# Down matrices of the experts started from ScalarE's queue instead of the sync engine's

## What is computed

```python
weights = (g_w * e_w).reshape(-1)                       # 2 experts per token
expert = (g_idx * EXPERTS_PER_GROUP + e_idx).reshape(-1)
order = jnp.argsort(expert)
xs = t[order // EXPERT_TOPK]                            # 512 slots, sorted by expert
sizes = jnp.bincount(expert, length=N_EXPERTS)
hid = jax.nn.silu(lax.ragged_dot(xs, w_gate, sizes)) * lax.ragged_dot(xs, w_up, sizes)
out = lax.ragged_dot(hid, w_down, sizes) * weights[order][:, None]
```

## Time and profile before

| | us |
|---|---|
| median of 3 runs | 1532.62 (1530.26 to 1532.73) |
| the profiled execution | 1532.07 |
| its span in the trace | 1530.3 |
| TensorE busy (matmuls) | 1366.8, 89% |
| VectorE busy | 529.9, 35% |
| ScalarE busy | 359.4, 23% |
| GpSimd busy | 54.2, 4% |
| moved by the DMA engines | 360.95 MB, 236 GB/s over the span |

### The profile page before, as it was taken

The page is one execution under the profiler, slowest core; times in us unless marked ns, Lnnn a source line. Parts: engine busy times, 40 slices in busy tenths (PEclk is TensorE's granted clock), DMA queues, the critical chain, the costliest instruction groups (busy, mean ns, idle before and its releaser), DMA issues.

```text
span 1530.3 us, 19672 instructions
## 1 busy us (share of the span) xinstructions
PE 1366.8 (89%) x7747; PEld 1010.1 (66%) x7748; DVE 529.9 (35%) x890; ACT 359.4 (23%) x500; POOL 54.2 (4%) x93
## 2 busy tenths in 40 slices
PE   6978999989979699998799788958999999888887
PEld 5867999987647499998676567854444444333335
DVE  2563554436654254543302434242111111111111
ACT  2632433320243243331301354022000000000001
POOL 1000000000110100000000000000000000000010
PEclk9989999999999899999999899978999999999998
DMA  9634555438871745450834113140999999999992
GB/s 311 235 110 165 166 166 197 158 99 326 318 277 54 248 165 165 164 192 1 362 140 164 47 63 110 55 176 1 419 429 428 429 428 429 429 428 429 428 428 96
DMA packets 101168, 360.95 MB, mean 236 GB/s; under 512 B 4416, under 2 KB 51696, under 8 KB 88704
## 3 DMA queue, kind: packets, MB, share of 16 engines
q1 hardware_dynamic: 93344, 333.72, 56.4%
q0 software_dynamic: 7632, 26.44, 5.0%
q10 hardware_dynamic: 144, 0.11, 0.0%
HBM read 359.18 MB, written 1.07 MB: 235 GB/s over the span
## 4 chain that ended last, share of the span: by engine, by line
PE 71%; DMA 15%; DVE 9%; ACT 3%; issue 1%; POOL 0%; SPq 0%; POOLq 0%; DVEq 0%; ACTq 0%
PE ps L1380 17%; PE ps L1328 14%; DMA wbuf<-in_w_up 12%; PE ps L1647 10%; PE ps L1312 9%; PE ps L1659 4%; PE ps L1541 3%; PE ps L1319 3%; PE ps L1635 2%; DVE wbuf L999 2%; PE ps L1291 1%; DMA wbuf<-in_lru_w_in 1%; PE ps L1622 1%; DMA wbuf<-in_w_ada 1%; PE ps L1347 1%
## 5 line engine op out<-in xcount | busy, mean ns | idle before, releaser
L1380 PE MATMUL ps<-big_parts,parts 128*128 128x256 f32 x2112 | 261.8, 286 | 8.6 <-DVE big_parts L925 8.5
L1380 PEld LDWEIGHTS ps<-big_parts,parts 128*128 128x128 f32 x2112 | 259.2, 194 | 10.0 <-issue 9.3
L1647 PE MATMUL ps<-wbuf,big 128*64 128x512 f32 x1024 | 226.4, 593 | 14.2 <-DMA wbuf<-in_w_up 13.6
L1312 PE MATMUL ps<-big,wbuf 128*128 128x256 f32 x896 | 199.1, 385 | 11.8 <-DMA wbuf<-in_lru_w_in 4.6
L925 DVE TENSOR_TENSOR parts<-wbuf,parts 128x2048 fp32r<-128x2048 f32 x66 | 150.9, 2292 | 142.0 <-ACT parts L620 77.6
L1312 PEld LDWEIGHTS ps<-big,wbuf 128*128 128x128 f32 x896 | 172.8, 193 | 38.4 <-issue 9.4
L1647 PEld LDWEIGHTS ps<-wbuf,big 128*64 128x64 f32 x1024 | 84.6, 137 | 152.1 <-issue 145.8
L1328 PE MATMUL ps<-big_parts,parts 128*128 128x256 f32 x1056 | 134.1, 288 | 8.8 <-DVE parts L925 8.8
L1328 PEld LDWEIGHTS ps<-big_parts,parts 128*128 128x128 f32 x1056 | 131.9, 197 | 9.2 <-DVE parts L925 9.2
L1659 PE MATMUL ps<-wbuf,big 128*64 128x512 f32 x512 | 116.9, 597 | 19.5 <-DVE big L1257 19.5
L1255 DVE TENSOR_TENSOR big<-big,ps 128x256 f32<-128x256 f32 x32 | 13.5, 421 | 334.1 <-ACT big L814 334.1
(11 more groups left out here) (263 smaller groups left out, 1078.9 us busy)
## 6 DMA issues: line engine op xcount, KB each, us to landing
wbuf<-in_w_gate SPq DMA_DIRECT2D x32, 2048.0 KB, 25.2
wbuf<-in_w_up SPq DMA_DIRECT2D x32, 2048.0 KB, 29.6
wbuf<-in_w_down SPq DMA_DIRECT2D x32, 2048.0 KB, 29.3
wbuf<-in_ffn_w_in SPq DMA_DIRECT2D x44, 1024.0 KB, 9.4
wbuf<-in_w_ada POOLq DMA_DIRECT2D x12, 2048.0 KB, 12.0
wbuf<-in_ffn_w_out SPq DMA_DIRECT2D x22, 1024.0 KB, 5.1
wbuf<-in_w_in SPq DMA_DIRECT2D x10, 2048.0 KB, 8.0
wbuf<-in_attn_w_qkv SPq DMA_DIRECT2D x6, 2048.0 KB, 11.0
```

The lines of the kernel that those rows point to most:

```text
L1312: ins = mm(b[:, d * 256:(d + 1) * 256], w[:, k, (m + d) * P:(m + d + 1) * P], rhs[:, k], start=(k == 0), stop=(k == kn - 1))
L1380: ins = mm(ps[:, b, d * 256:(d + 1) * 256], w[pw][:, k, d * P:(d + 1) * P], h_part_of[px][:, k], start=(k == 0 and i == 0), stop=(k == KC ...
L1647: ins = mm(at, x[:, k], gu_place[s][:, :, k, h * 256:(h + 1) * 256], start=(k == 0), stop=(k == KC - 1))
```

## The change

The three down loads of `load_next` in SP's loop, and the two behind it, are taken out, together with SP's waits for `down_done`. ScalarE starts them instead, right behind its copy L816 of the same expert's result; the copy has waited for the same `down_done`. For that ScalarE's loop gets three experts in its body (slots are fixed addresses there too), nine times round for experts 0 to 26, and five experts written out behind it, the last three without a load. Gate and up stay with SP, and so do all three matrices of experts 0 to 2.

```diff
@@ -459,8 +459,6 @@
                 sp.wait_ge(gu_done[0], e + 1 + EXPERT_SLOTS)
                 load_gate_up(sp, s, e + EXPERT_SLOTS)
-                sp.wait_ge(down_done[0], e + 1)
-                load_down(sp, s, e + EXPERT_SLOTS)
@@ -817,12 +815,21 @@
             nc.scalar.nop().then_inc(y_ev[0], 1)
-            with act.Fori(0, N_EXP) as e:
+
+            def act_expert(e, s):
                 n_more, before_more = more_windows(act, e)
                 with act.If(n_more > 0), act.Fori(0, n_more) as w:
                     act_window(1, before_more + w)
                     act.wait_ge(more_done, before_more + w + 1)
                 act_window(0, e)
+                if s is not None:
+                    load_down(act, s, e + EXPERT_SLOTS)
+
+            with act.Fori(0, (N_EXP - EXPERT_SLOTS) // EXPERT_SLOTS) as j:
+                for s in range(EXPERT_SLOTS):
+                    act_expert(EXPERT_SLOTS * j + s, s)
+            for e in range(N_EXP - N_EXP % EXPERT_SLOTS - EXPERT_SLOTS, N_EXP):
+                act_expert(e, e % EXPERT_SLOTS if e + EXPERT_SLOTS < N_EXP else None)
```

## The result

The changed kernel takes 1538.36 us (median of 6 runs, 1536.1 to 1539.6), the one before 1531.78 in its 6 runs (1526.9 to 1532.73). The ratio, which is formed over all runs and not from the two medians, is 1.0045 with a 95% interval of 1.0031 to 1.0059: **slower**, by 4.7 to 9.0 us. The forecast was 1541.0, slower by 8.6 in the expert stage, within 1534 to 1547.

The account below looks back on a forecast made before the run. The expert stage's unbroken DMA stream was taken to bound the kernel. Terms 0 + 0 + 8.6 + 0 on 1532.07 us gave 1540.7, or 1541.2 against the median; forecast 1541.0 us, range 1534 to 1547.

Parts of the forecast that it names:

- What bounds the kernel: Expert stage: the DMA stream of weights never pauses, 14.68 us an expert; TensorE needs less, 13.43.
- (b): Expert stage: the later down issues open no hole in the stream; last matrix still lands about 1500.8; cost 0.
- The sum for the last byte: End of the expert stream: 1495 + 1.325/0.4285 puts the last byte at 1498.1 us.
- (a): Issue of downs on ScalarE: 0.6 to 0.7 us later, behind L816, covered by 6.27 us; cost 0, SP's saving 0.
- (c): Landing order: two queues share engines half and half, a down takes 9.8 us; downs run ahead, ups fall behind.
- The rival of one stream in effect: Both issuers' loads served in order asked for, down 31 landing last; not slower, 1532.1 to 1532.7 us; chance 0.12.
- (d): Stage end: up 31 lands last, 5.0 us later; TensorE's 13.43 pace after up 30 makes the last L1647 +8.6 us.
- just in time: Stage end: down 31, issued at 1476.1, is through at 1490.5, before up 30 lands at 1491.0.
- (e): Stream rate with two queues: bounded at +6.4 to -3.0 us on 425.8 us; taken as 0.
- the tail stays: Behind the last L1647: the work on TensorE, VectorE and ScalarE keeps its length.

Follow-up runs that it names:

- swap: Against the changed kernel, queues exchanged: ScalarE starts gate and up, SP starts down; 1539.50 us, ratio 1.0052 to the kernel before.
- last1: Against the kernel before, only the down load of expert 31 is moved to ScalarE's queue; 1536.09 us, ratio 1.0030.
- last2: Against the kernel before, only the down loads of experts 30 and 31 are moved to ScalarE's queue; 1540.88 us, ratio 1.0050.

## Why the prediction was right

**What bounds the kernel, and (b), no hole.** Right. The sum for the last byte gives 1498.1 in both traces.

**(a) The issue costs nothing.** Right, and sooner than expected. It does not stand behind the 0.60 us of the copy; ScalarE's rows of the changed kernel:

```profile
1157.37 0.60 ACT L814 ACTIVATE big<-ps 128x512 f32<-128x512 f32 x1 [6.17 <-PE ps L1666]
1157.51 0.35 ACTq L385 DMA_DIRECT2D wbuf<-in_w_down  x1
1164.24 0.38 ACT L812 ACTIVATE big<-ps 128x256 f32<-128x256 f32 x1 [6.27 <-PE ps L1654]
```

It begins 0.14 us after the copy begins, some 0.2 us later than SP's did and not 0.6 to 0.7, takes 0.35 instead of 0.41, and the next silu has its 6.27 us of idle time as in the earlier trace rows.

**(c) Half and half.** Right, nearly: 13.9 us of flight where 1.9 + 9.8 + 2.7 = 14.4 were expected, and swap shows the same with the roles exchanged. The queues show it directly, here while the last down flows (after, 1479.4 to 1488.6 us):

```profile
q1 hardware_dynamic: 146, 2.13, 54.4%
q10 hardware_dynamic: 126, 1.80, 46.0%
```

In last1, from 1469 to 1478 us, it is 1.87 MB on q1 and 2.03 on q10. This was the step with the thinnest evidence, a pair of one software and one hardware queue in short packets. The rival of one stream in effect fell with it. The Trainium skill's rule (DMA: Bandwidth & Descriptors, Issuing engines are not separate DMA queues) is that issuing from several engines saves only the issuer's time. For the rate the traces agree, 428 GB/s either way; for the time they do not, the order of landing was worth 8.4 us.

**(d) 5.0 us for the last landing, 3.6 for TensorE's pace.** Right in both parts and their sum: up 30 at 1490.84 (1491.0 expected), last product at 1504.42 (1504.5). last1 and last2 were to separate them and do so in kind; in size each has some of the lower clock in it. The check that down 31 is through "just in time" held too: it was issued at 1475.3.

**(e) The rate.** The bounds of +6.4 and -3.0 us were wide for nothing; the value taken, 0, was right.

**The total** was 2.6 us high. 0.6 of it is the kernel before, which the forecast put at 1541.0 - 8.6 = 1532.4 and whose median over six runs is 1531.78. The other 2.0 are that stage and time differ: +8.4 in the stage, +6.6 in the medians (4.7 to 9.0 by the interval). In the two profiles the spans differ by 6.8 us, the stage's 8.4 less 1.7 for the tail and 0.1 more ahead of the stage. The step "the tail stays" is the one that was loose. The tail has two lengths, 34.3 and 32.7 us, by when TensorE's clock falls in it, and the profile of before happens to have the long one. Which kernel gets which, and how often, these profiles of one execution each do not settle.

No version here beats the kernel before. The stream's 425.8 us are full in every one, and its last 4.9 us are already hidden in the order gate, up, down; the wait left in front of the last product in the earlier trace rows is 1.03 us.

## What to carry to other kernels

When the transfers bound a stage, putting some of them on a second queue adds no bandwidth but changes the order in which they land: queues that both had work shared the engines nearly in halves here (rows of one length on both), so the one with fewer bytes runs ahead, and what is needed first can become what lands last. Look at the last landings of the stage and at what each releases; keep the matrix with the shortest work behind it for the end. Waits in the middle cost nothing, provided that the consumer has enough steps left to work them off at the difference of the two paces (here 1.25 us an expert, against a debt of nearly 10: with the last eleven downs back in the old order it was gone, with the last two it was not).

## What was not expected of the hardware

A single wait of TensorE of 5.9 or 7.8 us for a load was followed by a stretch at granted clock 0.50, in which the gate-and-up product took 9.48 and 9.10 us instead of 7.09. A wait of 2.08 us did the same in last2: the clock was 1.00 from 1478 to 1488 us and 0.50 from 1490 to 1492, and the product took 8.77. The waits of about 1 us an expert left the product at 7.09 in every kernel:

```profile
1478.00:1480.00 2.00, 2.00 (x12) 0.77 (x10) 0.00 (x0) 0.00 (x0) 0.00 (x0) 1.00 1.00 426
1490.00:1492.00 2.00, 2.00 (x6) 0.68 (x7) 0.00 (x0) 0.00 (x0) 0.00 (x0) 0.50 1.01 426
```

So each of these three longer waits cost 1.7 to 2.4 us beyond its length, which the same waiting in pieces of 1 us did not.
